# Tiles of two products turned inside the product ahead, and a feed-forward fed by the unnormed residual

## The reference

```python
g_nsa, g_dn = jnp.split(jax.nn.sigmoid(merge_g), 2, axis=-1)
mixed = g_nsa * (o_nsa @ w_up_nsa[l]) + g_dn * (o_dn @ w_up_dn[l])
x = x + mixed @ w_o[l]
h2 = rms_norm_2(x, norm2_w[l])        # x * rsqrt(mean(x*x) + eps) * w
x = x + (jax.nn.silu(h2 @ w_ffn_gate[l]) * (h2 @ w_ffn_up[l])) @ w_ffn_down[l]
return rms_norm_2(x, norm_f_w)
```

## Time and profile before

| | before |
|---|---|
| median of 3 runs (lowest, highest) | 2649.36 us (2648.11, 2660.02) |
| the profiled execution: its time, its span | 2648.88 us, 2647.0 us |
| granted TensorE clock, mean | 0.961 |
| busy: PE, PEld | 2454.6 us (93%), 2113.3 us |
| busy: DVE, ACT, POOL | 1486.4 us (56%), 1256.8 us (47%), 18.3 us |
| mean DMA rate | 154 GB/s |

### The profile page before, as it was taken

The page is one execution under the profiler, slowest core; times in us unless marked ns, Lnnn a source line. Parts: engine busy times, 40 slices in busy tenths (PEclk is TensorE's granted clock), DMA queues, the critical chain, the costliest instruction groups (busy, mean ns, idle before and its releaser), DMA issues.

```text
span 2647.0 us, 37575 instructions
## 1 busy us (share of the span) xinstructions
PE 2454.6 (93%) x13892; PEld 2113.3 (80%) x13892; DVE 1486.4 (56%) x2566; ACT 1256.8 (47%) x2304; POOL 18.3 (1%) x38
## 2 busy tenths in 40 slices
PE   6999798799999899998799989889899999999997
PEld 5888546678777699876587868778799999998886
DVE  4555544556455544787376666565555555555554
ACT  4545424555455544554355343554544444444443
POOL 1000000000000000000000000000000000000000
PEclk9999899899999999999699999999999999999999
DMA  5666404456443546655254232555456666666554
GB/s 170 192 193 194 127 1 134 136 153 176 133 120 128 175 130 183 188 155 160 80 159 136 80 96 72 189 170 182 143 177 189 183 182 182 181 183 206 192 186 156
DMA packets 246458, 408.53 MB, mean 154 GB/s; under 512 B 29920, under 2 KB 62752, under 8 KB 245440
## 3 DMA queue, kind: packets, MB, share of 16 engines
q1 hardware_dynamic: 242608, 392.15, 49.1%
q0 software_dynamic: 3152, 10.59, 1.1%
q10 hardware_dynamic: 576, 4.19, 0.4%
HBM read 400.59 MB, written 6.29 MB: 154 GB/s over the span
## 4 chain that ended last, share of the span: by engine, by line
PE 46%; DVE 4%; ACT 2%; issue 1%; DVEq 0%; ACTq 0%
PE banks L311 7%; PE banks L313 7%; PE banks L312 7%; PE banks L304 6%; PE banks L305 6%; PE banks L306 6%; DVE weights_low L283 1%; PE banks L1420 1%; PE banks L1718 1%; PE banks L1710 1%; PE banks L1717 1%; ACT weights_high L280 1%; PE banks L561 0%; PE banks L718 0%; DVE residual L2208 0%
## 5 line engine op out<-in xcount | busy, mean ns | idle before, releaser
L283 DVE TENSOR_TENSOR weights_low<-weight_ring,weights_high 128x512 fp32r<-128x512 f32 (+2 forms) x1512 | 1004.2, 676 | 883.5 <-ACT weights_high L280 872.2
L280 ACT CAST weights_high<-weight_ring 128x512 fp32r<-128x512 f32 (+2 forms) x1512 | 910.4, 609 | 1091.7 <-PE banks L313 698.0
L311 PE MATMUL banks<-weights_high,hidden_T_high 128*128 128x512 f32 x1568 | 632.9, 404 | 25.3 <-DVE weights_low L283 21.2
L312 PE MATMUL banks<-weights_low,hidden_T_high 128*128 128x512 f32 x1568 | 617.5, 394 | 0.0
L313 PE MATMUL banks<-weights_high,hidden_T_low 128*128 128x512 f32 x1568 | 617.4, 394 | 0.0
L304 PE MATMUL banks<-hidden_T_high,weights_high 128*128 128x256 f32 (+2 forms) x1840 | 524.5, 285 | 15.3 <-DVE weights_low L283 15.2
L305 PE MATMUL banks<-hidden_T_low,weights_high 128*128 128x256 f32 (+2 forms) x1840 | 522.6, 284 | 0.0
L306 PE MATMUL banks<-hidden_T_high,weights_low 128*128 128x256 f32 (+2 forms) x1840 | 522.5, 284 | 0.0
L311 PEld LDWEIGHTS banks<-weights_high,hidden_T_high 128*128 128x128 f32 x1568 | 298.9, 191 | 97.2 <-issue 13.8
L304 PEld LDWEIGHTS banks<-hidden_T_high,weights_high 128*128 128x128 f32 (+2 forms) x1840 | 351.5, 191 | 18.7 <-DVE weights_low L283 9.5
L305 PEld LDWEIGHTS banks<-hidden_T_low,weights_high 128*128 128x128 f32 (+2 forms) x1840 | 351.5, 191 | 0.7
(11 more groups left out here) (359 smaller groups left out, 1858.2 us busy)
## 6 DMA issues: line engine op xcount, KB each, us to landing
weight_ring<-in_w_in SPq DMA_DIRECT2D x168, 512.0 KB, 3.6
weight_ring<-in_w_gla_in SPq DMA_DIRECT2D x96, 512.0 KB, 3.7
weight_ring<-in_w_gate SPq DMA_DIRECT2D x88, 512.0 KB, 3.6
weight_ring<-in_w_ffn_up SPq DMA_DIRECT2D x88, 512.0 KB, 3.7
weight_ring<-in_w_down SPq DMA_DIRECT2D x88, 512.0 KB, 4.5
weight_ring<-in_w_mla_in SPq DMA_DIRECT2D x48, 512.0 KB, 3.7
weight_ring<-in_w_gla_out SPq DMA_DIRECT2D x32, 512.0 KB, 4.2
weight_ring<-in_w_mla_out SPq DMA_DIRECT2D x32, 512.0 KB, 4.3
```

Source lines behind the costliest of these rows:

```text
L280: nc.scalar.copy(hi, raw).then_inc(high_ready, 1)
L283: nc.vector.tensor_tensor(lo, raw, hi.bitcast(F32), ALU.subtract).then_inc(low_ready, 1)
L311: pe.matmul(out, ahi[:, ts_], hi, start=(k == 0), stop=False)
L312: pe.matmul(out, ahi[:, ts_], lo, start=False, stop=False)
```

## The change

- `prod_up` becomes one round of eight chunks written out; `prod_o` one round of four. VectorE's sums come as before, and `merged` goes.
- `turn_mix`: two groups are turned before the fifth tile of each of up chunks 3, 5 and 7, the last two before tile 3 of the first output chunk, once all sums are done. ScalarE and VectorE make the high and low parts after every second split in chunks 6 and 7, each only when the old tile in its place was used (the new `free`).
- `turn3` now reads X itself. Two groups are turned before tile 8 of output chunks 1, 2 and 3 (X of the chunk ahead is there), the last two before feed-forward tile 2. The copies are made late in the last output chunk.
- `norm3` only makes the inverse roots `stat_3`, in the side steps of the first feed-forward chunk. Two diagonal matrices times a matrix of ones (PE) and a copy (ACT) spread them over the partitions as `scale_row`.
- The gate chunk is evicted by VectorE with a multiply by `scale_row`; ScalarE's SiLU then runs in place on SBUF, one instruction of 1024 columns. The up chunk stays unscaled; `add_residual` of `prod_down` multiplies by `stat_3` instead.
- The squares of the residual go to a junk piece of SBUF instead of bank 4.

```diff
@@ Halve.scalar_steps
                 nc.scalar.wait_ge(turned, self.turned0 + g + 1)
+                if self.free is not None:
+                    nc.scalar.wait_ge(split_used, self.free(g))
@@ products and turns
-        prod_up = Product([(A["w_up"][0], 8, 0, W, W, hidden, False),
-                           (A["w_up"][1], 8, 0, W, W, lambda k: hidden(NSA_H + k), False)], D // W)
+        prod_up = Product([(A["w_up"][n], 8, i * W, 0, W, (hidden, lambda k: hidden(NSA_H + k))[n], False)
+                           for i in range(ROUNDS) for n in range(2)])
-        turn_mix = Halve(lambda t, k: mixed[:, t, k * P:(k + 1) * P], KD, hidden)
-        prod_o = wide(A["w_o"], KD, 4, 0, hidden)
+        turn_mix = Halve(lambda t, k: mixed[:, t, k * P:(k + 1) * P], KD, hidden, free=lambda g: last_up + 2 * g + 2)
+        prod_o = Product([(A["w_o"], KD, n * W, 0, W, hidden, False) for n in range(4)])
+        turn3 = Halve(lambda t, k: X[:, t, k * P:(k + 1) * P], KD, hidden, lambda k: small["norm2"][:, k:k + 1],
+                      free=lambda g: last_o + 2 * g + 2)
+        AHEAD = 6
@@ up_tensor
+                elif c % 2 == 1 and k == 4:
+                    i = c // 2 - 1
+                    pe.wait_ge(sum_done, i + 1)
+                    for g in (2 * i, 2 * i + 1):
+                        turn_mix.turn_group(pe, g)
@@ new functions
+        def o_tensor(pe):
+            def before(n, k):
+                if (n, k) == (0, 3):
+                    pe.wait_ge(sum_done, ROUNDS)
+                    for g in range(AHEAD, KD // 2):
+                        turn_mix.turn_group(pe, g)
+                if n == 0:
+                    pe.wait_ge(low_out, turn_mix.first + k // 2 + 1)
+                elif k == 8:
+                    prod_o.wait_chunk(pe, n - 1)
+                    for g in (2 * n - 2, 2 * n - 1):
+                        turn3.turn_group(pe, g)
+            prod_o.tensor(pe, before)
+        def o_side(mixes, turns):
+            pace = Pace()
+            yield from pace.to(2)
+            yield from pace.run(mixes)
+            for g in range(AHEAD):
+                yield from pace.to(3 * KD + 2 * g + 2)
+                next(turns)
+        def ffn_tensor(pe):
+            def before(n, k):
+                if (n, k) == (0, 2):
+                    prod_o.wait_chunk(pe, 3)
+                    for g in range(AHEAD, KD // 2):
+                        turn3.turn_group(pe, g)
+                if (n, k) == (0, 12):
+                    pe.wait_ge(diag_ready, 1)
+                    for t in range(NT):
+                        last = pe.matmul(ps[:, 4, t * P:(t + 1) * P], ones, scale_diag[:, t, :], start=True, stop=True)
+                    last.then_inc(row_made, 1)
+                if n == 0:
+                    pe.wait_ge(low_out, turn3.first + k // 2 + 1)
+            prod_ffn.tensor(pe, before)
+        def ffn_side_scalar(turns):
+            pace = Pace()
+            yield from pace.to(1)
+            yield from pace.run(turns)
+            yield from pace.run(norm3.scalar_steps(), 2)
+            yield from pace.to(12)
+            nc.scalar.wait_ge(row_made, 1)
+            nc.scalar.copy(scale_row, ps[:, 4, 0:S]).then_inc(row_ready, 1)
+        def ffn_side_vector(turns):
...
+            yield from pace.run(turns)
+            yield from pace.run(norm3.vector_steps(), 3)
+            for t in range(NT):
+                V(v.tensor_scalar(scale_diag[:, t, :], ident, stat_3[:, t:t + 1], None, ALU.mult))
+            v.sem_inc(diag_ready, 1)
@@ ffn_scalar
-                for t in range(2):
-                    last = nc.scalar.activation(gateT[:, 2 * t:2 * t + 2, :], two(b, t), ACT.Silu)
-                return last
+                nc.scalar.wait_ge(chunk_evicted[c0 % 2], i + c0 // 2 + 1)
+                nc.scalar.activation(gateT, gateT, ACT.Silu).then_inc(ffn_bounded, 1)
+                return None
@@ ffn_vector
+                if n == 0:
...
+                    for t in range(2):
+                        last = v.tensor_tensor(gateT[:, 2 * t:2 * t + 2, :], two(b, t), row, ALU.mult)
+                    return last
+                v.wait_ge(ffn_bounded, i + 1)
@@ add_residual
-                    last = nc.vector.tensor_tensor(x, ps[:, b + t, :], x, ALU.add)
+                    last = nc.vector.tensor_tensor(x, ps[:, b + t, :], x, ALU.add) if scale is None else \
+                        nc.vector.scalar_tensor_tensor(out=x, in0=ps[:, b + t, :], scalar=scale[:, t:t + 1], in1=x,
+                                                       op0=ALU.mult, op1=ALU.add)
```

196 lines of the change are left out of this document (103 added, 93 removed).

## The result

The changed kernel takes **2627.4 us** (median of 6 runs, 2626.5 to 2634.0), the kernel before in the same comparison 2648.5 us (6 runs, 2647.0 to 2660.0): ratio 0.9921, 95% interval 0.9900 to 0.9941. The forecast was 2627, within 2622 to 2635.

What follows compares the result with a forecast made beforehand. TensorE, busy 2454.6 of 2647.0 us, was taken as the bound, so its gaps were to win. Terms 9.9 + 13.7 - 0.8 - 0.5 = 22.3 us off 2648.9 gave 2626.6, stated as 2627; range 2622 to 2635.

Steps and rivals of the forecast that it cites:

- part 1: Turning mixed tiles inside the up product removes 14.0 us, adds 3.5 for pairs and 0.6 waiting: gain 9.9 us.
- the second gap: TensorE's wait from the last output product matmul to the first feed-forward matmul, 11.58 us, costing 11.46, all to go.
- slow clock: Slow matmuls after the second hole of each gap: 1.69 us in the output product, 1.53 in the feed-forward.
- small matmuls: Two matmuls in the feed-forward that spread the inverse roots over partitions: 0.3 us, between 0 and 0.6.
- first gate round: SiLU's table load behind the wait for VectorE makes the first gate chunk late: 0.8 us once, with restart.
- residual add: Down product's scaled adds cost 0.06 us more each, two in each of four chunks: 0.5 us, between 0 and 1.
- The gaps: TensorE's waits after the up product and after the output product, start to start: 7.98 and 11.46 us.
- A pair of groups: Two transpose groups turned between tiles: four pairs 4.0 us at 0.5 a group, 3.2 if restarts are shared; 3.5 taken.
- The wait for the last sum: Last mixed pair, in the output product: sum ready after 4.7 us, three tiles fill 4.1, wait 0.6 at most.
- Group 4 of the mixed tiles: In the last up chunk ScalarE waits before TensorE's fifth tile, casts queued behind: counted 0, up to 0.5 us.
- The gate boundary: In each feed-forward round ScalarE's SiLU and casts wait for VectorE's gate eviction: 0.7 us left, cost 0.
- rival of a late boundary each round: Every gate chunk stalls about 0.5 us in 11 feed-forward rounds, 5.5 us more: 2632 us; chance 0.13.

Runs made afterwards that it cites:

- e1: Kernel before with only the mixed tiles turned inside the up product, norm, X turns, gate and residual as before: 2646.3 us, ratio 0.9982.
- e2: Kernel before with only X turned in the output product, gate scaled by VectorE and residual scaled; up product as before: 2637.7 us, ratio 0.9961.
- e8: Changed kernel with residual squares later, SiLU's table loaded early and the last mixed pair turned before output tile 4 instead of 3: 2622.6 us.
- e6: Changed kernel with a one-column SiLU behind the square root, so its table load comes early: 2632.3 us, ratio 0.9927 to the kernel before.
- e5: Changed kernel with three unread ScalarE copies (about 1.9 us) behind SiLU in each of 11 rounds: 2643.3 us, ratio 0.998 to the kernel before.
- e4: Changed kernel with one unread ScalarE copy (about 0.5 us) behind SiLU in each round: 2632.7 us, ratio 0.9919 to the kernel before.
- e7: Changed kernel with ScalarE's residual squares made one by one behind later casts, not ahead of them: 2631.2 us, ratio 0.992 to the kernel before.
- e3: Kernel before with unread matmuls filling the two long gaps after the up and output products: 2646.2 us, ratio 0.9977.

## Why the prediction was right, step by step

The working went by terms that can be put beside the columns of the table. That the median came within 0.4 us of the forecast says less than the columns do: in an execution with a late M all that follows lies 5 to 10 us later, and how many of six are late is nothing that the prediction knew.

| column | predicted | measured |
|---|---|---|
| M to O: part 1, and three pairs of X at 0.875, the price taken | -9.9 + 2.6 = -7.3 | -7.2 |
| O to F: the second gap | -11.5 | -11.35 |
| F to D: groups, hole and slow clock gone; a pair, small matmuls, first gate round | -6.0 + 0.9 + 0.3 + 0.8 = -4.0 | -3.9 |
| D to end: residual add | +0.5 | +0.55 |
| sum | -22.3 | -21.9 |

- **The gaps** as whole distances, start to start, were the right thing to price: they went wholly, and in e1 and e2 each on its own.
- **A pair of groups.** I took 3.5 us for four pairs, between 4.0 and 3.2. Read as above they cost 0.88 each, 3.5 in all. But the reason for the lower end was wrong. A single group in the kernel before, TensorE in order of time:

```profile
1774.50 0.40 PE L313 MATMUL banks<-weights_high,hidden_T_low 128*128 128x512 f32 x1
1774.74 0.60 PE L561 MATMUL banks<-constants,projections 128*128 128x128 f32 x4
1775.09 0.49 PE L311 MATMUL banks<-weights_high,hidden_T_high 128*128 128x512 f32 x1
1775.41 0.39 PE L312 MATMUL banks<-weights_low,hidden_T_high 128*128 128x512 f32 x1
```

From 1774.50 to 1775.41 it took 0.91 us where two normal steps are 0.45, so one group costs 0.46 us, and a pair at 0.88 is at most 0.04 below two of them: hardly any of the restart is shared, where the lower end supposed 0.2. My 0.5 a group, from the whole stretch of 6.74 us, held other small losses of the product's start as well. So 3.5 us for four pairs was right by a wrong split, and that it lay midway was in part luck.
- **The wait for the last sum**, "0.6 us at most", was 0.6; e8 removed it.
- **Group 4 of the mixed tiles.** ScalarE stood for 2.54 us before it, as the instruction order said, and TensorE did not notice, as counted:

```profile
1762.89 0.65 ACT L596 CAST hidden_T_high<-banks 128x256 fp32r<-128x256 f32 x2 [2.54 <-PE banks L561]
```

- **Small matmuls** are the term that was mis-sized most: 0.45 us, taken 0.3 from a nearest row of four transposes, within its 0 to 0.6. **First gate round**: 0.83 us start to start, taken 0.8; e6 got 0.8 of it back.
- **The gate boundary**: room 0.7 us predicted, 0.64 by e5, none of it used up by the new handovers. The rival of a late boundary each round had 13% and was nearer than its mechanism looks: half a microsecond of extra work was still free (e4), two were not (e5).
- **The residual add** costs 0.063 us more each, against 0.062 from the earlier trace rows, and the whole column 0.55 against 0.5.
- **Not in the sum:** the squares write to SBUF instead of a bank, and 512 columns take 0.632 us where they took 0.602. They stand in the path of the stalls that e7 removed. But e1 has these squares with the plain adds, and its D to end is 254.98 us, 0.03 above the kernel before: the 0.55 is the scaled adds' alone.
- **The step that decides the distance** from the last up matmul to the first feed-forward matmul: 114.1 before, about 93 predicted. The last up matmul lies 18 steps of 0.227 ahead of 1772.44, at 1768.35; 1861.23 - 1768.35 = 92.9.

What the prediction had wrong lay outside its sum. It took the slow clock to be only in the steps after the holes; e3 and the granted clock showed that the 16 transposes behind each gap ran at the lower level as well. That cost was in the sum all the same, since the gaps were taken from start to start, transposes included.

## What to carry to other kernels

Price a gap from the last matmul ahead to the first one behind, with all that runs slowly in it, and price what stands in its place from single groups of the same shape; then the sum holds even where its inner split is wrong. Before a wait is put ahead of a queue of casts or loads, compute the room from the last cast ahead to the first use behind: 0.6 us of room was enough, and work put in beyond it came out at full price in every round. What stays after a large change is often a short stall at each chunk boundary, where an engine's side work stands ahead of its casts; put it behind them.

## What the runs showed of the hardware

- Right behind idle gaps of 4.5 and 8.0 us the transposes ran at the lower clock level (granted clock 0.50): 3.55 and 3.48 us for 16, against 1.97 with the gaps filled. Shorter holes of 2.2 and 2.5 us soon behind were followed by about 1.6 us of loss each.
- 1.2 us of idle time in each of ten rounds of 47.5 us, and 2.53 us in the first, left the granted clock at 1.00 (e5). So did the 0.3 us waits of the down product. So the length of a hole alone does not decide: one of 2.2 us was followed by the lower level even with the gap ahead filled (e3).
- Stages that do the same work end up to 12 us apart between executions (M from 1711.5 to 1723.4), and the late ones have the lower mean granted clock up to M, 0.94 against 0.95; from M on the same kernel repeats within 0.05 us. For a change in the last third of a kernel, distances from a mark decide what medians of six runs do not.
- A scaled add from a bank (0.744 us for 512 columns) costs 0.063 us more than a plain one (0.681), and a square of 512 columns written to SBUF (0.632 us) 0.03 more than one written to a bank (0.602).
- A table load on ScalarE takes 1.28 us, with 0.02 us between the cast ahead and its start and 1.29 us from its start to the next activation (e6).
